# One core, two chained transformer blocks: front-stage loads begun from three queues, the mixer's small matmuls put between the wide passes, and sparse attention's units taken head by head

## The reference, cut to what matters

```
hn = rmsnorm(h, norm1_g[l])
proj = hn @ w_in[l]
u, q, k, v, g_ssm, g_att = jnp.split(proj, SPLITS, axis=-1)
y_ssm = s5_mixer(u, ssm_a_re[l], ...)      # 32 groups of 16 channels, a 64-wide complex state each, scanned over time
q = rmsnorm(q.reshape(...), q_norm_g[l]) * q_scale
...
o = gb[..., 0:1] * o_cmp + gb[..., 1:2] * o_slc + gb[..., 2:3] * o_win   # sparse attention: three softmax branches
```

## Time and profile before

| what | us |
|---|---|
| median of 3 runs (2568.82 to 2572.18) | 2569.73 |
| the profiled execution | 2566.05 |
| its span, first to last instruction | 2564.3 |
| front stage, up to the first instruction of the next | 0 to 239.94 |
| sparse attention, first matmul to the next stage's first | 1917.57 to 2130.65 |

### The profile page before, as it was taken

One profiled execution on the slowest core, in us unless ns is written; L12 is line 12 of the kernel. 1 busy time (PEld: TensorE's weight loads), 2 busy tenths in 40 slices (PEclk: granted clock), 3 DMA queues, 4 the chain that ended last, 5 costly groups with the idle time before them and its releaser, 6 DMA issues. The chain is left out here.

```text
span 2564.3 us, 29257 instructions
## 1 busy us (share of the span) xinstructions
PE 2175.6 (85%) x11628; PEld 1805.3 (70%) x11628; DVE 1388.6 (54%) x1959; ACT 919.6 (36%) x1342; POOL 111.3 (4%) x167
## 2 busy tenths in 40 slices
PE   2898889989999898999564999659979998559993
PEld 2897589978999786863353888547968777548882
DVE  4962632626554545312443999654136664459995
ACT  3452353221010005310222777431124561437772
POOL 0432000000000000000001000000000000010000
PEclk9987589989999998985585999879875799569997
DMA  5332022314222222210124999822430001069993
GB/s 154 93 86 50 0 68 98 118 42 105 92 84 83 82 83 79 91 50 0 35 69 156 350 397 401 295 75 72 117 84 1 1 1 66 19 216 385 395 396 132
DMA packets 170071, 328.42 MB, mean 128 GB/s; under 512 B 39809, under 2 KB 104481, under 8 KB 169809
## 3 DMA queue, kind: packets, MB, share of 16 engines
q1 hardware_dynamic: 126800, 281.47, 31.1%
q0 software_dynamic: 9520, 27.43, 3.4%
q10 hardware_dynamic: 33616, 17.65, 2.7%
HBM read 301.29 MB, written 19.99 MB: 125 GB/s over the span
## 5 line engine op out<-in xcount | busy, mean ns | idle before, releaser
L2013 PE MATMUL ps<-m_ws,m_xbT 128*128 128x512 f32 x1344 | 318.8, 394 | 2.8 <-DVE m_xbT L2178 2.8
L2013 PEld LDWEIGHTS ps<-m_ws,m_xbT 128*128 128x128 f32 x1344 | 255.4, 190 | 56.9 <-DVE m_xbT L2178 3.6
L2171 DVE TENSOR_TENSOR m_ws<-ring,m_ws 128x2048 fp32r<-128x2048 f32 x112 | 255.8, 2289 | 33.6 <-ACT m_ws L2063 31.5
L1493 PE MATMUL ps<-ffT,ff_ws 128*128 128x264 f32 (+1 forms) x1056 | 241.2, 323 | 4.7 <-DVE ff_ws L409 4.7
L2063 ACT CAST m_ws<-ring 128x2048 fp32r<-128x2048 f32 x112 | 213.3, 1910 | 77.9 <-PE ps L2013 48.3
L1493 PEld LDWEIGHTS ps<-ffT,ff_ws 128*128 128x128 f32 x1056 | 176.4, 190 | 20.4 <-DVE ff_ws L409 4.8
L1493 PE MATMUL ps<-ffT_lo,ff_ws 128*128 128x264 f32 (+1 forms) x528 | 170.1, 322 | 0.0
L2039 PE MATMUL ps<-m_ws,m_hT 128*128 128x512 f32 x672 | 166.8, 397 | 0.0
L1291 PE MATMUL ps<-hT,mx_ws 128*128 128x264 f32 x768 | 143.4, 287 | 7.3 <-DVE mx_ws L196 6.4
L2039 PEld LDWEIGHTS ps<-m_ws,m_hT 128*128 128x128 f32 x672 | 122.2, 188 | 23.1
L2168 DVE TENSOR_TENSOR m_ws<-ring,m_ws 128x2048 fp32r<-128x2048 f32 x56 | 128.2, 2290 | 8.6 <-ACT m_ws L2061 7.7
(11 more groups left out here) (463 smaller groups left out, 4182.2 us busy)
## 6 DMA issues: line engine op xcount, KB each, us to landing
ring<-in_moe_w_gate SPq DMA_DIRECT2D x112, 512.0 KB, 5.4
ring<-in_moe_w_up SPq DMA_DIRECT2D x112, 512.0 KB, 7.5
ring<-in_moe_w_down SPq DMA_DIRECT2D x56, 1024.0 KB, 8.3
ring<-in_w_up SPq DMA_DIRECT2D x22, 1024.0 KB, 5.1
ring<-in_w_in SPq DMA_DIRECT2D x16, 1024.0 KB, 6.5
ring<-in_gla_w_in SPq DMA_DIRECT2D x12, 1024.0 KB, 5.1
ring<-in_w_down SPq DMA_DIRECT2D x11, 1024.0 KB, 4.9
ring<-in_nsa_w_in SPq DMA_DIRECT2D x10, 1024.0 KB, 7.3
```

Source lines behind the costliest of these rows:

```text
L1493: ins = nc.tensor.matmul(ps[:, bank, 0:b - a], w[j][:, k, s * P:(s + 1) * P], x[l][:, k, a:b], start=(k == 0 and j == l), stop=(k == KD - ...
L2013: ins = nc.tensor.matmul(ps[:, it % 2, :], xbT[:, blk % 2, a, 4 * half + k, :].bitcast(F32R), v[b][:, k, :], start=(half == 0 and k == 0 a ...
L2171: ins = V.tensor_tensor(o, x.rearrange("p (j k w) -> p j k w", k=4, j=2), x0, ALU.subtract)
```

## The change

In the front stage the ACT queue issues only the three loads for the mixer's decay; the loads for its output matrices (`c_loads`) and the norm's gain go to SP, ahead of the weights, and the others to POOL. The small matmuls are written as generators: `order` names with a wide item the small ones that are issued between its matmuls, one by one in even shares. The values are done in ten items of one half width each. A new buffer `xs` takes the state increments out of PSUM by an ACT copy, and DVE's order changes: the second pair of V and R matrices is made before the table E, and the splits of slabs come earlier. In sparse attention one line sets another order of the units.

```diff
-            order = [("p", 0), ("p", 1), ("p", 2), ("p", 3), ("p", 4), ("v", 0), ("p", 5), ("m", 0), ("k", 0), ("x", 0), ("p", 6), ("m", 1),
...
+            order = [("p", 0), ("p", 1), ("p", 2), ("p", 3), ("p", 4, ("v", 0)), ("p", 5, ("x", 0)), ("m", 0), ("p", 6, ("k", 0), ("v", 1)),
+                     ("m", 1), ("p", 7, ("x", 1)), ("m", 2), ("p", 8, ("k", 1)), ("m", 3), ("p", 9), ("m", 4), ("p", 10, ("y", 0)), ("m", 5),
+                     ("p", 11, ("v", 2), ("x", 2)), ("m", 6), ("t", 0, ("k", 2)), ("m", 7), ("t", 1, ("y", 1)), ("t", 2, ("v", 3)),
+                     ("t", 3, ("x", 3)), ("t", 4), ("t", 5, ("k", 3)), ("t", 6), ("t", 7, ("y", 2)), ("t", 8), ("t", 9)]
...
+                                    n_pass += 1
+                                    if n_pass == 48:
+                                        ins.then_inc(proj_done, 1)
+                                    while n_step * 48 < total * n_pass:
+                                        next(pieces)
+                                        n_step += 1
...
+                for _ in piece("y", 3):
+                    pass
...
-                act.dma_start(g1, A["norm1_g"][0].partition_broadcast(P)).then_inc(g_in, 16)
                 for to, frm in a_loads:
                     act.dma_start(to, frm).then_inc(a_in, 16)
-                for to, frm in c_loads:
-                    act.dma_start(to, frm).then_inc(c_in, 16)
...
+                    elif what == "x":
+                        act.wait_ge(x_done, i + 1)
+                        if i:
+                            act.wait_ge(x_read, i)
+                        nc.scalar.copy(xs[:].rearrange("p (a c) -> p a c", a=2), ps[:, 4:6, 0:264]).then_inc(x_out, 1)
...
+                for to, frm in lam_loads:
+                    pool.dma_start(to, frm).then_inc(lam_in, 16)
+                for to, frm in b_loads:
+                    pool.dma_start(to, frm).then_inc(b_in, 16)
...
+                S.lo(dve, 2)
                 build_v(0)
                 build_r(0)
-                S.lo(dve, 2)
-                dve.wait_ge(r_built, 1)
+                S.lo(dve, 3)
+                build_v(1)
+                build_r(1)
+                dve.wait_ge(r_built, 2)
...
+                    if n == 32:
+                        S.lo(dve, 4)
+                scan(0)
+                build_v(2)
+                S.lo(dve, 5)
...
-            units = [(hd, i) for i in range(TT) for hd in range(NH)]
+            units = [(hd, i) for hd in range(NH) for i in (0, 3, 1, 2)]
```

More of the change, by code:

```diff
@@ L8 @@
 from contextlib import ExitStack, contextmanager
+import itertools
 import math
@@ L659, in _, with piece @@
                 pe.wait_ge(low, 2 * len(TILES1))
[L660 to L691, removed]
+                def piece(what, i):
+                    U = uT[:, i].rearrange("p (g n) -> p g n", g=8)
+                    if what == "v":
                         pe.wait_ge(vt_built, i + 1)
@@ L699, in _ @@
                                 ins = nc.tensor.transpose(ps[:, 4 + part, P * j:P * j + P], vp[:, part, j, :], ident[:])
-                        ins.then_inc(vt_done, 1)
+                                if part and j == 3:
+                                    ins.then_inc(vt_done, 1)
+                                yield
+                    elif what == "x":
+                        pe.wait_ge(vt_out, 2 * i + 2)
+                        pe.wait_ge(u_in[i], 16 * C8)
+                        for part in range(2):
+                            for j in range(4):
+                                for g in range(2):
+                                    q = slice(64 * g, 64 * g + 64)
+                                    ins = nc.tensor.matmul(ps[q, 4 + part, NB8 * j:NB8 * j + NB8], VT[:, part, j, q], U[:, 2 * j + g, :],
+                                                           start=True, stop=True)
+                                    if part and j == 3 and g:
+                                        ins.then_inc(x_done, 1)
+                                    yield
                     elif what == "k":
@@ L780, in _ @@
                 S.hi(act, 1)
-                for what, i in order:
+                for what, i in moves:
                     if what in "pmt":
@@ L1095, in _ @@
                     n += w_
-                S.lo(dve, 3)
-                for i in range(4):
-                    if i < 3:
-                        build_v(i + 1)
-                        dve.wait_ge(vt_built, i + 2)
-                    else:
-                        S.lo(dve, 7)
-                    scan(i)
-                    if i < 3:
-                        build_r(i + 1)
-                        S.lo(dve, i + 4)
+                    if n == 32:
[3 more added lines that the diff above has]
+                S.lo(dve, 5)
+                dve.wait_ge(vt_built, 3)
+                scan(1)
+                build_r(2)
+                S.lo(dve, 6)
+                build_v(3)
+                dve.wait_ge(vt_built, 4)
+                S.lo(dve, 7)
+                scan(2)
+                build_r(3)
+                scan(3)
             @block.sync
```

115 lines of the change are left out of this document (78 added, 37 removed), and 3 rows, old and new, of the table order.

## The result

The changed kernel took 2601.07 us (median of four runs), the kernel before 2569.28: ratio 1.012, 95% interval 1.0095 to 1.0147. It is slower, where I had forecast 2507 and faster. One of the four runs, at 3257 us, was disturbed and is left out of the ratio; the median of the other three is 2598.70. The profiled execution took 2598.70 us, 32.65 more than that of before.

A forecast was written before the change was run, and what follows sets the result against it. The start was taken as bound by ACT's queue order, the front stage and sparse attention by PE, partly at half clock. 2566 - 24 - 8 - 31 = 2503, or 2507 on the median's scale; 8-in-10 range 2489 to 2545.

The forecast's parts named there:

- What a woven step costs: Front stage: small matmuls issued singly between wide ones cost +8 to -6 us over the stage, taken as 0.
- its weight load hides under the wide matmul: Front stage: the favourable side of weaving, a woven step's weight load is covered, and a y saves 1 to 2 us.
- granted clock over 0.95 in it: Front stage, from first wide pass to next stage: sign that PE's clock stays above 0.95, against windows of 0.80 to 0.88.
- 8 us saved: Front stage after the first wide pass: weaving and new orders end its work at 171 instead of 179.1 us, bounds 0 and 14.
- 24 us saved: Kernel start: loads from three queues bring the first wide pass from 59.05 to 35 us, bounds 21 and 26.
- the trap with GpSimd's descriptors: Start: a skill rule that GpSimd transfers' descriptors cannot be written while VectorE runs in two-port mode; under 1 us expected.
- a clock that stays low: Sparse attention, rival: all mixed heads run at 1.2 GHz, 19.1 us each, 94 us slower, 2631 in sum; chance 0.08.
- it falters for two or three heads: Sparse attention, rival: clock drops for a few heads, or DVE's turns make a head 11.5 us: 2525; chance 0.14.
- The term "31": Sparse attention head by head: 33 us saved (179 against 212), taken as 31; bounds 15 and 36 if the clock holds.
- 10.4 a head: Sparse attention: period of a mixed head at full clock, 9.7 us of PE plus some 0.7 of waiting; 166 for sixteen.
- the hold on i = 3: Sparse attention: in each head PE waits some 0.7 us for DVE and ACT ahead of the transposes of i = 3.
- weaving costs instead: Front stage, rival: wide pieces stall in their middle and concurrency is lost, -8 instead of +8 and some: 2523; chance 0.12.

The follow-up runs named there:

- e4_full_tiles: Changed kernel, everything woven, but each x, k and y matmul on all 128 rows and columns of the array (values not the reference's): 2529.56 us, ratio 0.9856.
- e8_big_first: Kernel before with the three-queue loads and sparse attention's units ordered i = 3, 2, 1, 0, each for all heads: 2514.11 us (single run).

## Why the prediction was wrong

**The step that failed** is "What a woven step costs", where I wrote "I take 0", with bounds of +8 and -6 us. It measured +59 us against the same items standing whole (253.3 against 194.2 us), and +71 us against weaving with full tiles (182.5). I had seen in the earlier trace rows that grouped x matmuls run two at a time, and priced the loss of that (the estimate by the Trainium skill, TensorEngine Tiling (Array Packing), Overview, was 8 to 9 us for x and k; the lost concurrency of x alone came to some 10, so the page was nearer than my 0). What I had as a certainty was the other half: "its weight load hides under the wide matmul". That holds for V, whose tile is the full array, and for no other kind: 0.235 us a full x step, 0.47 one on half the columns, 0.57 one on half the rows. The rows had a sign of it. In a y item PE goes from T, a full tile, to two R of 64 rows and back, and I read 0.95 us for such a triple. The last y of e4_full_tiles stands whole too, with R on the full array (timeline of PE):

```profile
200.15 0.39 PE L724 MATMUL ps<-uT,fr_T 128*128 128x66 f32 x2
...
200.82 0.39 PE L724 MATMUL ps<-uT,fr_T 128*128 128x66 f32 x2
```

A triple takes 0.67 us there with as many matmuls, so by this reading 0.28 of the 0.95 were the two changes of shape. I took the 0.95 as the work itself. The bounds had no right to be narrow: 160 woven part-tile steps at even 0.2 us are 32 us.

The Trainium skill has the rule that speaks against this edit, in the list of key properties of the same page that I cited for the concurrency (TensorEngine Tiling (Array Packing), Tiling Modes): "Changing tiling mode (not just tile) drains the TensorE". By it x (128x64), k (128x32) and R (64x128) between full matmuls change the mode twice a visit and V and T not at all. The runs agree: full shape 0.235 us, 64 columns 0.47, and two matmuls in the same mode on different halves 0.48; that a drain is what happens, and not only that the weight load begins late, they do not show. The page gives no price. I had used its second property and passed over its first.

**The clock of the front stage.** I had "granted clock over 0.95 in it". It was 0.84, and 0.55 over p10. With the items whole it was 0.88, and bundled but woven, with the same shapes, 0.94; with full tiles it was 0.99, though there the y matmuls themselves were on the full array too. So the mechanism I hoped for, that weaving holds the clock up, exists; it was the single visits to part tiles, those of y above all, that undid it.

**The orders without the weaving.** "8 us saved" was 14.6 lost: 194.2 us with the new order unwoven against 179.6 with the old one. Idle time ahead of the next stage was 15.2 us, where I had put the way home of the last y at 10 without cover, and was 1.8 before: 13.4 of the 14.6. With full tiles woven the stage was 182.5 against the 173 forecast, 5 us of it that tail.

**The loads**: "24 us saved" measured 22.25 in the changed kernel and about 22 alone. Right, step by step, down to DVE's first scaled tile at 19.25 (18 to 22 forecast). Nothing showed of the trap with GpSimd's descriptors that I had set against it: up to its first scaled tile, DVE's only wait for a load is 0.16 us, at 17.82.

**Head by head**: mechanism right, size wrong. The clock rises and mostly stays (0.98, 0.96), as forecast. The rival of a clock that stays low did not occur; the milder one, that it falters for two or three heads, did: three heads took 13.3 us instead of 11.7, 5 us in all. Against that the start at the lower clock, which I had put at 8 us, cost under 2. The term "31" measured 12.9 mainly because a head takes 11.7 us even at the full clock instead of "10.4 a head". The forecast allowed 0.7 us for the hold on i = 3; it is 1.23, largely since I had left ACT's copy of the transposes of the unit before out of that path, and i = 2 waits 0.41 as well. The larger part is in the short units: I priced them at half their length at 1.2 GHz, 1.06 and 1.89 us, as PE's own time. At full clock in e8_big_first an i = 1 unit takes 2.41 us and an i = 0 unit 1.7, 1.2 more together, and PE is busy for only 32.7 of 36.0 and 25.6 of 33.9 us: other engines pace them there, DVE, busy for 29.8 of the 33.9, most likely.

The rival "weaving costs instead" named the right place, and of its two mechanisms the lost concurrency was real; stalls in the middle of wide pieces were not the cause, since PE was idle for only 6 of 238 us. It had priced the whole at 16 us.

## What to carry to other kernels

Weave small matmuls into a wide pass only if they use the same part of the array; otherwise each visit to a part tile costs, so make visits few, and keep part tiles that run side by side together. Where light work runs at the lower clock, try the dense pieces ahead of it: the i = 1 units here then ran at the full clock, though the last i = 0 units did not always. Take the pace of a small matmul from start to start, never from a record's own time. A bound for a cost that no row shows must come from the number of times it is paid, not from the costs one has thought of.

## What the runs showed of the hardware

- A visit to a 64-column tile between full-array matmuls took 0.47 us for one matmul of 66 columns and 0.48 for two on different halves; on the full array a visit took 0.235. Part tiles' weight loads, and the next full one's, began no earlier than their matmuls; with full tiles they began up to 0.12 us earlier.
- A y triple (one full tile, two on 64 rows) took 0.95 us at the full clock, and 0.67 with all three on the full array.
- The i = 1 units of sparse attention ran at a granted clock of 1.00 behind long units and at 0.50 behind short ones: 2.41 against 3.80 us each. Which level this work got depended on what ran ahead of it.
- The same number of matmuls in the same places kept a granted clock of 0.99 with full tiles and 0.84 with part tiles.
